# Summing the modulation over partitions as two rows on the two column halves of TensorE, spread by DMA over a scratch in DRAM

## Chip, core and metric

The kernel runs on one core of a Trainium2 chip. The metric is the device time of one execution in microseconds (us). A core has TensorE (PE, matrix products), VectorE (DVE), ScalarE (ACT), GpSimd (POOL) and SyncE (SP); SP, ACT and POOL issue DMAs, which all run on the core's 16 DMA engines.

## The reference, cut to what matters

The program is three transformer layers on 256 tokens of width 1024. The first layer has two feed-forward networks (FFN 0 and 1); the second and the third have one each (FFN 2 and 3) and are modulated by a condition vector `c`:

```
cond = jax.nn.silu(c)
for i in range(DEPTH_2):
    mod = (cond @ ada_w[i] + ada_b[i])[:, None, :]
    sh1, sc1, g1, sh2, sc2, g2 = jnp.split(mod, 6, axis=-1)
    h = rmsnorm_2(x, norm1_g[i]) * (1.0 + sc1) + sh1
    ...
    x = x + g1 * y
    h = rmsnorm_2(x, norm2_g[i]) * (1.0 + sc2) + sh2
    x = x + g2 * swiglu_2(h, w_gate[i], w_up[i], w_down[i])
```

`mod` is 12 parts of 1024 numbers (two layers of six). Eight of them (shifts and scales) are used per channel and four (gates) multiply rows of tokens.

## The kernel before

**Weights.** All layers' weights stream in 190 units of 128x2048 numbers (1 MB). For each unit SP issues the load, ACT rounds it to fp32r (`hi`, L465), DVE computes the rest (`lo`, L1094), and PE multiplies with both: `hi*x_hi + hi*x_lo + lo*x_hi` (L1878 to L1887). ACT and DVE work four units (`AHEAD`) ahead of PE.

**Pairs.** An FFN has 11 pairs `p` of three units. In a pair PE does the gate and up products for both token tiles (`gate_up`, 48 matmuls of 512 columns), turns the hidden values of the pair before (`turn_hid`, L2010), multiplies them into the output (`down_all`, 24 matmuls), and then does `mod_job(p)` if there is one. `down_all` waits for `hid_lo` (L1254) of DVE, which waits for `hid_hi` (L542) of ACT.  The next pair's first matmul waits for `hid_done` of this pair.

**Modulation.** POOL loads `ada_w` in 96 slices of 128x1024. DVE's `ada(n)` (L1105, L1109) multiplies slice `n` by its column of `cond` and adds it to `ada_acc[:, q % 2, :]`; after eight slices each partition holds a partial sum of part `q`, and what is left is the sum over the 128 partitions. This is done in PSUM bank 3 at the pairs that `MOD_JOBS` names, half a part (512 columns) at a time, so there are 24 jobs in pairs 4 to 9 of FFN 0 and at like places in FFN 1 to 3 (the fourth part of each group falls in pairs 2 and 3 of the next FFN):

- a shift or a scale: four PE transposes of 128x128 (L2045), after which DVE sums along the row (L1124), so that the numbers come out one per partition, and adds the bias (L1128);
- a gate: ACT rounds the whole `ada_acc` part to fp32r (L555), DVE computes the rest (L1274), PE multiplies both with a matrix of ones (L2040, L2041), so that all 128 partitions hold the sum, and DVE adds it to `gate` (L1120).

**Order.** Every engine's order is written out by hand, and engines meet at semaphores. `mod_ps` counts PE's jobs, `mod_read` DVE's reading of bank 3. A block's sum in front of a norm or a gated add is waited for by `modg_done` or `mod_read`, many pairs later.

Of the kernel before, what the change touches and what calls it, by code (L numbers as in the profile page):

```python
# [13 lines left out]
P = 128  # L14
T = 256
# [91 lines left out]
ADA_FROM, ADA_PAIRS = 2, 8  # L107
GATES = [q for q in range(ADA_PARTS) if q % 6 in GATE]
MOD_JOBS = {}
for _q in range(ADA_PARTS):  # L110
    _f, _i = _q // 4, _q % 4
    for _half in range(2):
        MOD_JOBS[(PAIRS * _f + 4 + 2 * _i if _i < 3 else PAIRS * (_f + 1) + 2) + _half] = (_q, _half)

# [74 lines left out]
def program(nc, inp, out):  # L189
    with ExitStack() as ctx:  # L190
# [28 lines left out]
        stat = sb("stat", [P, 3, 16])  # L219
        ones_r = sb("ones_r", [P, P], F32R)  # L220
        both = stat[:, 0, 12:16]
# [25 lines left out]
        xn = overlay("xn", 56 * T, [P, 2, D])  # L247
        acc_hi = overlay("acc_hi", 50 * T, [P, D], F32R)
        acc_lo = overlay("acc_lo", 56 * T, [P, D], F32R)
        y_tok = overlay("y_tok", 0, [P, 2, 16, HD])  # L250
# [45 lines left out]
        hi_ready, lo_ready, unit_done = sem("hi_ready"), sem("lo_ready"), sem("unit_done")  # L296
        ada_used, acc_hi_done, acc_lo_done, ones_set = sem("ada_used"), sem("acc_hi_done"), sem("acc_lo_done"), sem("ones_set")
        ident_in, const_in, dist_in, mask2_in = sem("ident_in"), sem("const_in"), sem("dist_in"), sem("mask2_in")
# [11 lines left out]
        proj_out, low_out = sem("proj_out"), sem("low_out")  # L310
        mod_ps, mod_read, mod_bias, modg_done = sem("mod_ps"), sem("mod_read"), sem("mod_bias"), sem("modg_done")
        up_done, value_done = sem("up_done"), sem("value_done")
# [56 lines left out]
        def ada_of_pair(g):  # L369
# [5 lines left out]
            return range(first, first + ADA_PER)  # L375

        def gate_of_pair(g):


            q, h = MOD_JOBS.get(g, (0, 1))  # L380
            return q if h == 0 and q % 6 in GATE else None

# [60 lines left out]
        def _(act):  # L443
# [5 lines left out]
            def late_inputs():  # L449
                act.activation(ones_r[:, :], ones, ACT.Copy).then_inc(ones_set, 1)  # L450
                act.dma_start(const[:, C_DIST:], inp["const"][:, C_DIST:]).then_inc(dist_in, 16)
                act.dma_start(sinks[:, :], inp["sinks"].partition_broadcast(P)).then_inc(sinks_in, 16)
                act.dma_start(pos_i[:, :], inp["positions"]).then_inc(pos_in, 16)
                for i, name in enumerate(("q_gain", "k_gain")):
                    act.dma_start(qk_gain[:, i, :], inp[name].partition_broadcast(P)).then_inc(sinks_in, 16)
                for i, q in enumerate(GATE):
                    act.dma_start(gate[:, i, :], inp["ada_b"][0][q * D:(q + 1) * D].partition_broadcast(P)) \
                        .then_inc(gate_in[i], 16)
# [65 lines left out]
            def ffn(f, n, then):  # L524
# [15 lines left out]
                def hid_hi_of(p, cols, count):  # L540
                    act.wait_ge(hidT_done, count)
                    act.activation(hid_hi[:, p % 2, cols], ps[:, 2, cols], ACT.Copy).then_inc(hidhi_done, 1)  # L542

                def pair(p):
                    ug, ud = ffn_gate(f, p), ffn_down(f, p - 1)
                    if p > 0:
                        hid_hi_of(p - 1, slice(0, 2 * T), hidT_count(f, p - 1) + 1)
                    hi(ug + AHEAD)
                    silu(p, 0)
                    silu(p, 1)  # L550
                    hi(ug + 1 + AHEAD)
                    q = gate_of_pair(f * PAIRS + p)
                    if q is not None:
                        act.wait_ge(ada_used, C * (q + 1))
                        act.activation(acc_hi[:, :], ada_acc[:, q % 2, :], ACT.Copy).then_inc(acc_hi_done, 1)  # L555
                    if p > 0:
                        hi(ud + AHEAD)

                u0 = BASE[f"ffn{f}"]
# [527 lines left out]
        def _(dve):  # L1087
# [9 lines left out]
            def ada(n):  # L1097

                q, k = n // C, n % C
                dve.wait_ge(ada_loaded[n % ADA_SLOTS], 16 * (n // ADA_SLOTS + 1))  # L1100
                acc = ada_acc[:, q % 2, :]
                if k == 0:
                    if q >= 2:
                        dve.wait_ge(mod_ps, 2 * (q - 1))
                    V.tensor_scalar(acc, ada_raw[:, n % ADA_SLOTS, :], cond[:, 0:1], None, ALU.mult) \  # L1105
                        .then_inc(ada_used, 1)
                else:
                    dve.wait_ge(ada_used, n)
                    V.scalar_tensor_tensor(acc, ada_raw[:, n % ADA_SLOTS, :], cond[:, k:k + 1], acc, ALU.mult,  # L1109
                                           ALU.add).then_inc(ada_used, 1)  # L1110

            def mod_job(q, h):

                layer, kind = q // 6, q % 6
                job = 2 * q + h
                dve.wait_ge(mod_ps, job + 1)
                if kind in GATE:
                    i = GATE.index(kind)
                    dve.wait_ge(gate_in[i], 16 * (layer + 1))
                    V.tensor_tensor(gate[:, i, half(h)], gate[:, i, half(h)], ps[:, 3, :], ALU.add) \  # L1120
                        .then_inc(mod_read, 1)
                    return
                part = slice(8 * kind + 4 * h, 8 * kind + 4 * h + 4)
                V.tensor_reduce(mod[:, layer, part], ps[:, 3, :].rearrange("p (t n) -> p t n", t=4), AX.X, ALU.add) \  # L1124
                    .then_inc(mod_read, 1)
                dve.wait_ge(mod_read, job + 1)
                bias = ada_bT[:, 48 * layer + part.start:48 * layer + part.stop]
                V.tensor_tensor(mod[:, layer, part], mod[:, layer, part], bias, ALU.add).then_inc(mod_bias, 1)  # L1128
                if kind in SCALE and h == 1:
                    which = SCALE.index(kind)  # L1130
                    dve.wait_ge(mod_bias, 8 * layer + 4 * which + 4)
                    V.scalar_tensor_tensor(mod_g[:, layer, which, :], mod[:, layer, 8 * kind:8 * kind + 8], 1.0,
                                           vec_t[:, 32 + 8 * layer + 16 * which:40 + 8 * layer + 16 * which], ALU.add,
# [99 lines left out]
            def ffn(f, n, then, factor=None, gated=None):  # L1233
# [23 lines left out]
                def modulation(p):  # L1257
                    if f * PAIRS + p in MOD_JOBS:
                        mod_job(*MOD_JOBS[f * PAIRS + p])

                def pair(p):
# [7 lines left out]
                    for k in units[0:1]:  # L1269
                        ada(k)  # L1270
                    q = gate_of_pair(f * PAIRS + p)
                    if q is not None:
                        dve.wait_ge(acc_hi_done, GATES.index(q) + 1)
                        V.tensor_tensor(acc_lo[:, :], ada_acc[:, q % 2, :], acc_hi[:, :].bitcast(F32), ALU.subtract) \  # L1274
                            .then_inc(acc_lo_done, 1)
                    for k in units[1:2]:
# [48 lines left out]
                if gated is not None:  # L1325
                    dve.wait_ge(mod_read, 2 * (6 * (f - 2) + GATE[1]) + 2)
                if then is not None and then not in UNSHIFTED:
# [42 lines left out]
            def rows_then(stage, n, gated=None):  # L1370
# [4 lines left out]
                if gated is not None:  # L1375
                    dve.wait_ge(mod_read, 2 * (6 + GATE[0]) + 2)
                    dve.wait_ge(modg_done, 4)
# [148 lines left out]
            def gqa():  # L1526
# [148 lines left out]
                lo(v0 + 4)  # L1675
                dve.wait_ge(mod_read, 2 * GATE[0] + 2)
                dve.wait_ge(modg_done, 2)
# [22 lines left out]
            def stick():  # L1700
# [80 lines left out]

                dve.wait_ge(mod_read, 2 * (6 + GATE[0]) + 2)
                dve.wait_ge(modg_done, 4)
# [88 lines left out]
        def _(pe):  # L1872
# [109 lines left out]
            def ffn(f, n, then):  # L1982
# [48 lines left out]
                def mod_job(p):  # L2031
                    if f * PAIRS + p not in MOD_JOBS:
                        return
                    q, h = MOD_JOBS[f * PAIRS + p]
                    pe.wait_ge(ada_used, C * (q + 1))
                    wait(pe, mod_read, 2 * q + h)
                    if q % 6 in GATE:
                        pe.wait_ge(ones_set, 1)
                        pe.wait_ge(acc_lo_done, GATES.index(q) + 1)
                        TE.matmul(ps[:, 3, :], ones_r[:, :], acc_hi[:, half(h)], start=True, stop=False)  # L2040
                        TE.matmul(ps[:, 3, :], ones_r[:, :], acc_lo[:, half(h)], start=False, stop=True) \  # L2041
                            .then_inc(mod_ps, 1)
                        return
                    for k in range(4):
                        m = TE.transpose(ps[:, 3, k * P:(k + 1) * P],  # L2045
                                         ada_acc[:, q % 2, h * HALF + k * P:h * HALF + (k + 1) * P], ident)
                    m.then_inc(mod_ps, 1)
# [586 lines left out]
```

## Time and profile before

| what | value |
|---|---|
| median of 3 runs (lowest to highest) | 1173.44 us (1173.38 to 1174.34) |
| the profiled execution's own time | 1174.04 us |
| its span, first to last instruction | 1172.2 us |
| PE busy | 1160.1 us, 99% |
| DVE busy | 820.6 us, 70% |
| ACT busy | 599.3 us, 51% |
| granted TensorE clock, mean | 0.999 of full |
| DMA moved | 253.66 MB, mean 216 GB/s |

The span runs from the first to the last instruction; the execution's own time has a little more around it. An engine that is busy for 99% of the span leaves no room for others to be the limit, except at the places where it waits. A PE matmul's duration in the rows holds its way through the array and overlaps the next one; what it costs is the distance from its start to the next one's start.

### The profile page before, as it was taken

To read this page: it belongs to the slowest core of one execution; us is meant where nothing else is said; L and a number is where in the kernel's file an instruction comes from. 1 tells how busy PE (TensorE), PEld (TensorE's weight loads), DVE (VectorE), ACT (ScalarE), POOL (GpSimd) and SP (SyncE) were. 2 spreads that over 40 slices of the span, in tenths; PEclk is the share of its full clock that TensorE was granted. 3 is DMA by queue.
4 is the path that set the end of the run, shared out by engine and by line. 5 is a ranking of instruction groups with operands and counts; after the bars stand their busy time and mean duration, and the time that the engine had idled before them with its cause. 6 is when DMAs were issued, how large, how long until landed. Compare 5 with 4: busy or idle time off the path is not lost. (4 is left out here: it accounts for less than half of the span.)

```text
span 1172.2 us, 15112 instructions
## 1 busy us (share of the span) xinstructions
PE 1160.1 (99%) x6140; PEld 978.5 (83%) x6140; DVE 820.6 (70%) x1051; ACT 599.3 (51%) x780; POOL 51.1 (4%) x101
## 2 busy tenths in 40 slices
PE   8999999999999999999999999999999999999998
PEld 6888888889989888888888888888888978888887
DVE  5777877456757657887898967788785658554544
ACT  7443356445566643353578544334565676433441
POOL 0011110000000001111000001111000000000000
PEclk9999999999999999999999999999999999999999
DMA  9888684554445578887624457887546405755530
GB/s 370 340 307 320 222 346 179 198 182 143 144 145 166 194 269 318 298 289 277 248 72 145 180 215 271 298 319 270 224 144 235 143 20 196 251 179 179 184 139 37
DMA packets 44421, 253.66 MB, mean 216 GB/s; under 512 B 5568, under 2 KB 5952, under 8 KB 20544
## 3 DMA queue, kind: packets, MB, share of 16 engines
q1 hardware_dynamic: 29088, 199.78, 46.9%
q0 software_dynamic: 13824, 50.34, 12.1%
q10 hardware_dynamic: 1440, 2.58, 0.6%
q8 instruction: 49, 0.80, 0.3%
q14 instruction: 20, 0.16, 0.0%
HBM read 251.63 MB, written 1.05 MB: 216 GB/s over the span
## 5 line engine op out<-in xcount | busy, mean ns | idle before, releaser
L1094 DVE TENSOR_TENSOR w_lo<-raw,w_hi 128x2048 fp32r<-128x2048 f32 x145 | 330.8, 2288 | 101.0 <-ACT w_hi L465 100.9
L465 ACT ACTIVATE w_hi<-raw 128x2048 fp32r<-128x2048 f32 x145 | 275.3, 1911 | 32.8 <-DMA raw<-in_w 32.6
L1885 PE MATMUL ps<-w_hi,h_parts 128*128 128x512 f32 (+1 forms) x720 | 284.2, 395 | 1.0 <-DVE h_parts L1218 0.5
L1887 PE MATMUL ps<-w_lo,h_parts 128*128 128x512 f32 (+1 forms) x720 | 277.8, 386 | 0.0
L1886 PE MATMUL ps<-w_hi,h_parts 128*128 128x512 f32 (+1 forms) x720 | 277.3, 385 | 0.0
L542 ACT ACTIVATE hid_hi<-ps 128x512 fp32r<-128x512 f32 (+1 forms) x48 | 27.0, 562 | 260.3 <-PE ps L2010 260.3
L1885 PEld LDWEIGHTS ps<-w_hi,h_parts 128*128 128x128 f32 x720 | 135.5, 188 | 27.7 <-DVE h_parts L1229 0.9
L1887 PEld LDWEIGHTS ps<-w_lo,h_parts 128*128 128x128 f32 x720 | 135.3, 188 | 27.9
L1886 PEld LDWEIGHTS ps<-w_hi,h_parts 128*128 128x128 f32 x720 | 135.8, 189 | 25.0
L1109 DVE SCALAR_TENSOR_TENSOR ada_acc<-ada_raw,cond,ada_acc 128x1024 f32<-128x1024 f32 x84 | 107.5, 1280 | 3.4 <-DMA ada_raw<-in_ada_w 1.2
L1094 DVE TENSOR_TENSOR lo_extra<-raw_extra,hi_extra 128x2048 fp32r<-128x2048 f32 x40 | 91.5, 2287 | 13.6 <-ACT hi_extra L465 13.5
L1885 PE MATMUL ps<-w_hi,hid_hi 128*128 128x512 f32 x248 | 96.8, 390 | 0.0
L1887 PE MATMUL ps<-w_lo,hid_hi 128*128 128x512 f32 x248 | 96.6, 389 | 0.0
L1886 PE MATMUL ps<-w_hi,hid_lo 128*128 128x512 f32 x248 | 96.5, 389 | 0.0
L1254 DVE TENSOR_TENSOR hid_lo<-ps,hid_hi 128x512 fp32r<-128x512 f32 (+1 forms) x48 | 31.0, 645 | 90.0 <-ACT hid_hi L542 89.9
L438 POOL DMA_DIRECT2D ada_raw<-in_ada_w x96 | 50.8, 530 | 781.8 <-DVE ada_acc L1109 392.8
L1885 PE MATMUL ps<-hi_extra,h_parts 128*128 128x512 f32 x208 | 82.5, 397 | 0.0
L1887 PE MATMUL ps<-lo_extra,h_parts 128*128 128x512 f32 x208 | 81.2, 390 | 0.0
L1886 PE MATMUL ps<-hi_extra,h_parts 128*128 128x512 f32 x208 | 81.0, 390 | 0.0
L465 ACT ACTIVATE hi_extra<-raw_extra 128x2048 fp32r<-128x2048 f32 x40 | 76.2, 1912 | 6.7 <-DMA raw_extra<-in_w 6.7
L1878 PE MATMUL ps<-h_parts,w_hi 128*128 128x256 f32 x240 | 69.6, 290 | 0.0
L1879 PE MATMUL ps<-h_parts,w_hi 128*128 128x256 f32 x240 | 67.9, 283 | 0.0
(236 smaller groups left out, 1686.7 us busy)
## 6 DMA issues: line engine op xcount, KB each, us to landing
raw<-in_w SPq DMA_DIRECT2D x146, 1024.0 KB, 4.9
ada_raw<-in_ada_w POOLq DMA_DIRECT2D x96, 512.0 KB, 5.2
raw_extra<-in_w SPq DMA_DIRECT2D x40, 1024.0 KB, 5.1
raw<-in_w SPq DMA_DIRECT2D x4, 256.0 KB, 5.9
gate<-in_ada_b ACTq DMA_DIRECT2D x2, 512.0 KB, 12.3
gate<-in_ada_b SPq DMA_DIRECT2D x2, 512.0 KB, 5.9
out_x<-x SPq DMA_DIRECT2D x4, 256.0 KB, 2.0
const<-in_const ACTq DMA_DIRECT2D x1, 768.0 KB, 8.1
```

The lines of the kernel that those rows point to most:

```text
L438: pool.dma_start(ada_raw[:, n % ADA_SLOTS, :], w[:, k, (q % 6) * D:(q % 6 + 1) * D]) \
L465: act.activation(w_hi[SLOT[u]], raw[SLOT[u]], ACT.Copy).then_inc(hi_ready, 1)
L542: act.activation(hid_hi[:, p % 2, cols], ps[:, 2, cols], ACT.Copy).then_inc(hidhi_done, 1)
L1094: V.tensor_tensor(w_lo[SLOT[u]], raw[SLOT[u]], w_hi[SLOT[u]].bitcast(F32), ALU.subtract) \
L1109: V.scalar_tensor_tensor(acc, ada_raw[:, n % ADA_SLOTS, :], cond[:, k:k + 1], acc, ALU.mult, ALU.add).then_inc(ada_used, 1)
L1254: V.tensor_tensor(hid_lo[:, p % 2, cols], ps[:, 2, cols], hid_hi[:, p % 2, cols].bitcast(F32), ALU.subtract).then_inc(hidlo_done, 1)
L1878: TE.matmul(dst, wh, x_hi, start=start, stop=False, skip_group_check=True)
L1879: TE.matmul(dst, wh, x_lo, start=False, stop=False, skip_group_check=True)
L1885: TE.matmul(dst, x_hi, wh, start=start, stop=False, skip_group_check=True)
L1886: TE.matmul(dst, x_lo, wh, start=False, stop=False, skip_group_check=True)
L1887: return TE.matmul(dst, x_hi, wl, start=False, stop=last, skip_group_check=True)
```

## The change

The sum over partitions becomes one job per part, 12 in all, at the first of the two pairs where the part's halves were before. PE multiplies `ada_acc` (true fp32, both halves of the row) by a 128x64 block of ones: columns 0 to 511 on the left 64 columns of the array (PSUM partitions 0 to 63 of bank 3), columns 512 to 1023 on the right 64 (partitions 64 to 127). ACT copies the bank to `mod_row` and issues a DMA of partitions 0 and 64, that is the whole row of 1024, into a DRAM tensor `mod_rows`. In the next pair ACT issues the DMA that brings it back: for shifts and scales number `128*k + p` to partition `p`, column `k` (1024 pieces of 4 bytes), for gates the whole row to each of the 128 partitions (512 KB). At that pair's end DVE waits for it (`mod_in`) and adds the bias, or adds the row to `gate`. The fp32r rounding for gates, `ones_r`, the transposes and the sums along the row go.

```
-    for _half in range(2):
-        MOD_JOBS[(PAIRS * _f + 4 + 2 * _i if _i < 3 else PAIRS * (_f + 1) + 2) + _half] = (_q, _half)
+    MOD_JOBS[PAIRS * _f + 4 + 2 * _i if _i < 3 else PAIRS * (_f + 1) + 2] = _q
...
+        gate_rows = overlay("gate_rows", 50 * T, [P, D])
+        mod_row = overlay("mod_row", 54 * T, [P, HALF])
+        scratch = nc.dram_tensor("mod_rows", (ADA_PARTS, D), F32).ap()
...
             def late_inputs():
-                act.activation(ones_r[:, :], ones, ACT.Copy).then_inc(ones_set, 1)
...
+                def send_mod(q):
+                    act.wait_ge(mod_ps, q + 1)
+                    wait(act, mod_sent, 16 * q)
+                    act.activation(mod_row[:, :], ps[:, 3, :], ACT.Copy).then_inc(mod_copied, 1)
+                    act.wait_ge(mod_copied, q + 1)
+                    act.dma_start(scratch[q].rearrange("(s n) -> s n", s=2), mod_row[0:P:P // 2, :]).then_inc(mod_sent, 16)
+
+                def fetch_mod(q):
+                    act.wait_ge(mod_sent, 16 * (q + 1))
+                    layer, kind = q // 6, q % 6
+                    if kind in GATE:
+                        act.dma_start(gate_rows[:, :], scratch[q].partition_broadcast(P)).then_inc(mod_in, 16)
+                    else:
+                        act.dma_start(mod[:, layer, 8 * kind:8 * kind + 8], scratch[q].rearrange("(k p) -> p k", p=P),
+                                      allow_slow_non_contiguous=True).then_inc(mod_in, 16)
+
                 def pair(p):
...
                     hi(ug + AHEAD)
+                    if f * PAIRS + p - 1 in MOD_JOBS:
+                        fetch_mod(MOD_JOBS[f * PAIRS + p - 1])
                     silu(p, 0)
                     silu(p, 1)
                     hi(ug + 1 + AHEAD)
-                    q = gate_of_pair(f * PAIRS + p)
-                    if q is not None:
-                        act.wait_ge(ada_used, C * (q + 1))
-                        act.activation(acc_hi[:, :], ada_acc[:, q % 2, :], ACT.Copy).then_inc(acc_hi_done, 1)
                     if p > 0:
                         hi(ud + AHEAD)
+                    if f * PAIRS + p in MOD_JOBS:
+                        send_mod(MOD_JOBS[f * PAIRS + p])
...
-            def mod_job(q, h):
+            def mod_job(q):
...
-                dve.wait_ge(mod_ps, job + 1)
+                dve.wait_ge(mod_in, 16 * (q + 1))
                 if kind in GATE:
                     i = GATE.index(kind)
                     dve.wait_ge(gate_in[i], 16 * (layer + 1))
-                    V.tensor_tensor(gate[:, i, half(h)], gate[:, i, half(h)], ps[:, 3, :], ALU.add) \
-                        .then_inc(mod_read, 1)
+                    V.tensor_tensor(gate[:, i, :], gate[:, i, :], gate_rows[:, :], ALU.add).then_inc(mod_done, 1)
                     return
-                part = slice(8 * kind + 4 * h, 8 * kind + 4 * h + 4)
-                V.tensor_reduce(mod[:, layer, part], ps[:, 3, :].rearrange("p (t n) -> p t n", t=4), AX.X, ALU.add) \
-                    .then_inc(mod_read, 1)
...
+                part = slice(8 * kind, 8 * kind + 8)
...
                 def modulation(p):
-                    if f * PAIRS + p in MOD_JOBS:
-                        mod_job(*MOD_JOBS[f * PAIRS + p])
+                    if f * PAIRS + p - 1 in MOD_JOBS:
+                        mod_job(MOD_JOBS[f * PAIRS + p - 1])
...
-                    q = gate_of_pair(f * PAIRS + p)
-                    if q is not None:
-                        dve.wait_ge(acc_hi_done, GATES.index(q) + 1)
-                        V.tensor_tensor(acc_lo[:, :], ada_acc[:, q % 2, :], acc_hi[:, :].bitcast(F32), ALU.subtract) \
-                            .then_inc(acc_lo_done, 1)
...
-                    q, h = MOD_JOBS[f * PAIRS + p]
+                    q = MOD_JOBS[f * PAIRS + p]
                     pe.wait_ge(ada_used, C * (q + 1))
-                    wait(pe, mod_read, 2 * q + h)
-                    if q % 6 in GATE:
-                        pe.wait_ge(ones_set, 1)
-                        pe.wait_ge(acc_lo_done, GATES.index(q) + 1)
-                        TE.matmul(ps[:, 3, :], ones_r[:, :], acc_hi[:, half(h)], start=True, stop=False)
-                        TE.matmul(ps[:, 3, :], ones_r[:, :], acc_lo[:, half(h)], start=False, stop=True) \
-                            .then_inc(mod_ps, 1)
-                        return
-                    for k in range(4):
-                        m = TE.transpose(ps[:, 3, k * P:(k + 1) * P],
-                                         ada_acc[:, q % 2, h * HALF + k * P:h * HALF + (k + 1) * P], ident)
+                    pe.wait_ge(const_in, 16)
+                    wait(pe, mod_copied, q)
+                    for h in range(2):
+                        m = TE.matmul(ps[h * HD:(h + 1) * HD, 3, :], ones[:, 0:HD], ada_acc[:, q % 2, half(h)],
+                                      start=True, stop=True, skip_group_check=True)
                     m.then_inc(mod_ps, 1)
```

The later waits on `mod_read` become waits on `mod_done`, which counts the 12 parts.

PE's row at the end of pair 4 of FFN 0, where part 0 has its first job, reads so before (the last matmuls of `down_all`, the job, the first of the next pair):

```order
L1885 MATMUL ps<-hi_extra_70,hid_hi 128x512
L1886 MATMUL ps<-hi_extra_70,hid_lo 128x512
L1887 MATMUL ps<-lo_extra_68,hid_hi 128x512
L2045 MATMUL ps<-const,ada_acc 128x128 [waits ada_used]
L2045 MATMUL ps<-const,ada_acc 128x128 x3
L1885 MATMUL ps<-w_hi,h_parts 128x512 [waits hid_done,lo_ready]
```

The same place in the changed kernel, where line numbers above the job are two higher (L1885 is L1887):

```order
L1887 MATMUL ps<-hi_extra_70,hid_hi 128x512
L1888 MATMUL ps<-hi_extra_70,hid_lo 128x512
L1889 MATMUL ps<-lo_extra_68,hid_hi 128x512
L2041 MATMUL ps<-ada_acc,const 64x512 [waits const_in,ada_used]
L2041 MATMUL ps<-ada_acc,const 64x512
L1887 MATMUL ps<-w_hi,h_parts 128x512 [waits hid_done,lo_ready]
```

Four transposes here and four in pair 5 have become the two matmuls here; pair 5 has none.

ACT's row around the boundary of pairs 4 and 5, before (the two last `hi` of pair 4, then pair 5):

```order
L465 ACTIVATE w_hi<-raw 128x2048 [waits w_loaded2]
L465 ACTIVATE w_hi<-raw 128x2048 [waits w_loaded3]
L542 ACTIVATE hid_hi<-ps 128x512 [waits hidT_done]
L465 ACTIVATE w_hi<-raw 128x2048 [waits w_loaded4]
L537 ACTIVATE silu_g<-ps,rstd 128x256 [waits hid_done,gu0_done]
```

The same place in the changed kernel (lines are eight lower here):

```order
L457 ACTIVATE w_hi<-raw 128x2048 [waits w_loaded2]
L457 ACTIVATE w_hi<-raw 128x2048 [waits w_loaded3]
L541 ACTIVATE mod_row<-ps 128x512 [waits mod_ps]
L543 DMA mod_rows<-mod_row 2x512 [waits mod_copied]
L534 ACTIVATE hid_hi<-ps 128x512 [waits hidT_done]
L457 ACTIVATE w_hi<-raw 128x2048 [waits w_loaded4]
L553 DMA mod<-mod_rows 128x8x1 [waits mod_sent]
L529 ACTIVATE silu_g<-ps,rstd 128x256 [waits hid_done,gu0_done]
```

The copy and the send stand ahead of `hid_hi`, the fetch ahead of the first `silu`.

## Rows read from the trace of the kernel before

**Rows 1.** The page: span, and PE's busy time, share and instructions.

```profile
span 1172.2 us, 15112 instructions
...
PE 1160.1 (99%) x6140; PEld 978.5 (83%) x6140; DVE 820.6 (70%) x1051; ACT 599.3 (51%) x780; POOL 51.1 (4%) x101
```

**Rows 2.** Waits: PE's longest; us in total, times, longest.

```profile
PE ps L1936 <- DMA x<-in_x: 5.1, 1, 5.1
```

**Rows 3.** Groups of PE by form: count, busy us, mean ns, idle before.

```profile
L2045 PE MATMUL ps<-const,ada_acc 128*128 128x128 f32 x64 | 9.6, 271 | 0.0
...
L2040 PE MATMUL ps<-acc_hi,ones_r 128*128 128x512 f32 x8 | 3.3, 407 | 0.0
```

**Rows 4.** Timeline of PE, a transposing job: start us, duration us, line.

```profile
89.48 0.39 PE L1887 MATMUL ps<-lo_extra,hid_hi 128*128 128x512 f32 x1
89.71 0.60 PE L2045 MATMUL ps<-const,ada_acc 128*128 128x128 f32 x4
...
90.38 0.40 PE L1886 MATMUL ps<-w_hi,h_parts 128*128 128x512 f32 x1
```

**Rows 5.** Timeline of PE around the first and the second gate job.

```profile
158.63 0.39 PE L1887 MATMUL ps<-w_lo,hid_hi 128*128 128x512 f32 x1
...
159.57 0.40 PE L1885 MATMUL ps<-w_hi,h_parts 128*128 128x512 f32 x1
...
176.17 0.39 PE L1887 MATMUL ps<-w_lo,hid_hi 128*128 128x512 f32 x1
...
176.86 0.39 PE L1885 MATMUL ps<-w_hi,h_parts 128*128 128x512 f32 x1
```

**Rows 6.** Timeline of PE, a visit to two column halves in fp32 (128*64).

```profile
930.08 0.28 PE L1879 MATMUL ps<-h_parts,w_hi 128*128 128x256 f32 x1
930.20 0.28 PE L1880 MATMUL ps<-h_parts,w_lo 128*128 128x256 f32 x1
930.41 0.65 PE L2413 MATMUL ps<-z_buf,qkv 128*64 128x256 f32 x4
930.90 0.39 PE L2417 MATMUL ps<-z_buf,qkv 128*64 128x128 f32 x4
931.21 0.39 PE L1878 MATMUL ps<-h_parts,w_hi 128*128 128x256 f32 x1
931.44 0.28 PE L1879 MATMUL ps<-h_parts,w_hi 128*128 128x256 f32 x1
```

**Rows 7.** Timeline of PE, both halves apart (probT one, soft the other).

```profile
318.48 0.38 PE L2187 MATMUL ps<-probT,qkv 128*64 128x256 f32 x1
318.48 0.38 PE L2187 MATMUL ps<-soft,qkv 128*64 128x256 f32 x1
...
318.91 0.27 PE L2191 MATMUL ps<-probT,qkv 128*64 128x128 f32 x1
```

**Rows 8.** Timeline of ACT, start of pair 5 of FFN 0.

```profile
96.28 0.60 ACT L542 ACTIVATE hid_hi<-ps 128x512 fp32r<-128x512 f32 x1 [7.72 <-PE ps L2010]
```

**Rows 9.** Timeline of DVE, end of pair 5 and start of pair 6.

```profile
112.10 0.68 DVE L1124 TENSOR_REDUCE mod<-ps 128x4 f32<-128x512 f32 x1
...
114.19 0.69 DVE L1254 TENSOR_TENSOR hid_lo<-ps,hid_hi 128x512 fp32r<-128x512 f32 x1 [1.22 <-ACT hid_hi L542]
```

**Rows 10.** Timeline of PE, the first matmul of `down_all` in pair 6.

```profile
118.84 0.39 PE L1885 MATMUL ps<-hi_extra,hid_hi 128*128 128x512 f32 x1
```

**Rows 11.** Timeline of ACT's queue: start and duration of two DMA issues.

```profile
35.16 0.55 ACTq L453 DMA_DIRECT2D pos_i<-in_positions  x1
...
36.71 0.33 ACTq L455 DMA_DIRECT2D qk_gain<-in_k_gain  x1
```

**Rows 12.** DMA issues: count, KB each, median us to landing.

```profile
gate<-in_ada_b ACTq DMA_DIRECT2D x2, 512.0 KB, 12.3
...
qk_gain<-in_k_gain ACTq DMA_DIRECT2D x1, 32.0 KB, 8.6
...
pos_i<-in_positions ACTq DMA_DIRECT2D x1, 1.0 KB, 7.8
```

More of the change, by code:

```diff
@@ L107 @@
 ADA_FROM, ADA_PAIRS = 2, 8
-GATES = [q for q in range(ADA_PARTS) if q % 6 in GATE]
 MOD_JOBS = {}
@@ L219, in program @@
         stat = sb("stat", [P, 3, 16])
-        ones_r = sb("ones_r", [P, P], F32R)
         both = stat[:, 0, 12:16]
@@ L247, in program @@
         xn = overlay("xn", 56 * T, [P, 2, D])
-        acc_hi = overlay("acc_hi", 50 * T, [P, D], F32R)
-        acc_lo = overlay("acc_lo", 56 * T, [P, D], F32R)
+        gate_rows = overlay("gate_rows", 50 * T, [P, D])
+        mod_row = overlay("mod_row", 54 * T, [P, HALF])
+        scratch = nc.dram_tensor("mod_rows", (ADA_PARTS, D), F32).ap()
         y_tok = overlay("y_tok", 0, [P, 2, 16, HD])
@@ L296, in program @@
         hi_ready, lo_ready, unit_done = sem("hi_ready"), sem("lo_ready"), sem("unit_done")
-        ada_used, acc_hi_done, acc_lo_done, ones_set = sem("ada_used"), sem("acc_hi_done"), sem("acc_lo_done"), sem("ones_set")
+        ada_used = sem("ada_used")
         ident_in, const_in, dist_in, mask2_in = sem("ident_in"), sem("const_in"), sem("dist_in"), sem("mask2_in")
@@ L310, in program @@
         proj_out, low_out = sem("proj_out"), sem("low_out")
-        mod_ps, mod_read, mod_bias, modg_done = sem("mod_ps"), sem("mod_read"), sem("mod_bias"), sem("modg_done")
+        mod_ps, mod_copied, mod_sent, mod_in = sem("mod_ps"), sem("mod_copied"), sem("mod_sent"), sem("mod_in")
+        mod_done, modg_done = sem("mod_done"), sem("modg_done")
         up_done, value_done = sem("up_done"), sem("value_done")
@@ L375, in ada_of_pair @@
             return range(first, first + ADA_PER)
-        def gate_of_pair(g):
-            q, h = MOD_JOBS.get(g, (0, 1))
-            return q if h == 0 and q % 6 in GATE else None
         @block.sync
@@ L1103, in ada @@
                     if q >= 2:
-                        dve.wait_ge(mod_ps, 2 * (q - 1))
+                        dve.wait_ge(mod_ps, q - 1)
                     V.tensor_scalar(acc, ada_raw[:, n % ADA_SLOTS, :], cond[:, 0:1], None, ALU.mult) \
@@ L1110, in ada @@
                                            ALU.add).then_inc(ada_used, 1)
-            def mod_job(q, h):
+            def mod_job(q):
                 layer, kind = q // 6, q % 6
-                job = 2 * q + h
-                dve.wait_ge(mod_ps, job + 1)
+                dve.wait_ge(mod_in, 16 * (q + 1))
                 if kind in GATE:
@@ L1119, in mod_job @@
                     dve.wait_ge(gate_in[i], 16 * (layer + 1))
-                    V.tensor_tensor(gate[:, i, half(h)], gate[:, i, half(h)], ps[:, 3, :], ALU.add) \
-                        .then_inc(mod_read, 1)
+                    V.tensor_tensor(gate[:, i, :], gate[:, i, :], gate_rows[:, :], ALU.add).then_inc(mod_done, 1)
                     return
-                part = slice(8 * kind + 4 * h, 8 * kind + 4 * h + 4)
-                V.tensor_reduce(mod[:, layer, part], ps[:, 3, :].rearrange("p (t n) -> p t n", t=4), AX.X, ALU.add) \
-                    .then_inc(mod_read, 1)
-                dve.wait_ge(mod_read, job + 1)
+                part = slice(8 * kind, 8 * kind + 8)
                 bias = ada_bT[:, 48 * layer + part.start:48 * layer + part.stop]
-                V.tensor_tensor(mod[:, layer, part], mod[:, layer, part], bias, ALU.add).then_inc(mod_bias, 1)
-                if kind in SCALE and h == 1:
+                V.tensor_tensor(mod[:, layer, part], mod[:, layer, part], bias, ALU.add).then_inc(mod_done, 1)
+                if kind in SCALE:
                     which = SCALE.index(kind)
-                    dve.wait_ge(mod_bias, 8 * layer + 4 * which + 4)
-                    V.scalar_tensor_tensor(mod_g[:, layer, which, :], mod[:, layer, 8 * kind:8 * kind + 8], 1.0,
+                    dve.wait_ge(mod_done, q + 1)
+                    V.scalar_tensor_tensor(mod_g[:, layer, which, :], mod[:, layer, part], 1.0,
                                            vec_t[:, 32 + 8 * layer + 16 * which:40 + 8 * layer + 16 * which], ALU.add,
@@ L1325, in ffn @@
                 if gated is not None:
-                    dve.wait_ge(mod_read, 2 * (6 * (f - 2) + GATE[1]) + 2)
+                    dve.wait_ge(mod_done, 6 * (f - 2) + GATE[1] + 1)
                 if then is not None and then not in UNSHIFTED:
@@ L1375, in rows_then @@
                 if gated is not None:
-                    dve.wait_ge(mod_read, 2 * (6 + GATE[0]) + 2)
+                    dve.wait_ge(mod_done, 6 + GATE[0] + 1)
                     dve.wait_ge(modg_done, 4)
@@ L1675, in gqa @@
                 lo(v0 + 4)
-                dve.wait_ge(mod_read, 2 * GATE[0] + 2)
+                dve.wait_ge(mod_done, GATE[0] + 1)
                 dve.wait_ge(modg_done, 2)
@@ L1780, in stick @@
                 y_lo(7)
-                dve.wait_ge(mod_read, 2 * (6 + GATE[0]) + 2)
+                dve.wait_ge(mod_done, 6 + GATE[0] + 1)
                 dve.wait_ge(modg_done, 4)
```

## The prediction

> **What bounds the kernel now.** I read the page first: PE is busy for 1160.1 of the 1172.2 us of the span [rows 1]. The reader is to see that about 12 us are all that PE could ever stop waiting for. The list of waits is next: PE's longest is 5.1 us for the first input, at the very start [rows 2]; nothing in the middle is of that size. So the time is PE's row of work, placed end to end, and the change is worth what it does to the length of that row, plus any wait that it newly gives to PE. DVE (70% busy) and ACT (51%) [rows 1] stand in the shadow of PE, and work taken from them is worth nothing.
>
> **What the removed PE work cost.** A job cannot be priced by its busy time, since matmuls overlap; I take distances between starts. Two fp32r matmuls of 512 columns and one more before them take 0.69 us from 176.17 to 176.86 [rows 5], so one is 0.23. A transposing job: from 89.48 to 90.38 are 0.90 us [rows 4], in which lie two ordinary matmuls (L1887 before, L1885 behind) of 0.23 each; the four transposes with what they do to their neighbours cost 0.44. There are 64 transposes [rows 3], that is 16 jobs: 7.0 us. A gate job: 8 of them [rows 3], seven at 0.46 and the first, where PE waited a little for the fp32r parts of `ada_acc`, at 0.94 less 0.23, or 0.71 [rows 5]: 3.9 us. Removed in all: **11.0 us**.
>
> **What the added PE work costs.** 12 jobs of two true-fp32 matmuls, 64 columns wide, 512 columns long, on the two halves. No such job with 512 columns is in the trace, but the form with 256 and 128 is, in both attention stages. First, how fast they stream: with both halves at work, two records of 256 columns on each half take 0.43 us, from 318.48 to 318.91 [rows 7]; that is four passes over 256 columns, and the two halves start at the same 318.48, so they run side by side and the second is free. 512 columns are twice that: 0.86 us a job. Second, what a visit to the halves costs beside streaming: from 930.20 to 931.44 are 1.24 us [rows 6]. In it lie two ordinary matmuls of 256 columns at 0.12 (930.08 to 930.20), streams of 256 columns (0.43) and of 128 (half of it, 0.215). 1.24 - 0.24 - 0.43 - 0.215 leaves 0.355 us: the array is let run empty on the way in and on the way out, and the weights of the first matmul on each side are not loaded under the one before. A job is 0.86 + 0.355 = 1.215 us, and 12 of them **14.6 us**.
>
> The Trainium skill, TensorEngine Tiling (Array Packing), section Key Properties, says that "Mode switching requires drain". The trace agrees with it by the 0.355 us of [rows 6]; the page gives no time for it. By the page's rule on concurrency alone, without the drain, the job would be 0.86 and the change a gain of 0.7 us; the trace has a price for the drain, and I use it.
>
> Bounds of a job: 0.86 us if the switches cost nothing here, which [rows 6] speaks against; 1.72 + 0.355 = 2.075 us if the halves take turns, which [rows 7] speaks against. The switching part itself may differ by the neighbours, which here are 512 columns long and not 256: after the transposes, L1885 also starts its follower late, within the 0.44 above, so a known part of such a loss is around 0.1. I let the job range from 1.12 to 1.31.
>
> **Sum.** 14.6 - 11.0 = +3.6 us on PE's row. The profiled execution took 1174.04 us with its span of 1172.2; it would take 1177.6. It lies 0.6 above the median of the runs, 1173.44, which is the spread between runs, so the median goes to **1177.0**.
>
> **What lies beside PE and is costed at nothing.** Twelve copies of 128x512 from PSUM on ACT, each like `hid_hi` at 0.60 us, and the issue of the send. They stand in front of `hid_hi` of the next pair. ACT had been idle for 7.72 us there, waiting for PE's turn of the hidden values [rows 8]. PE's job ends about when the 90.38 of [rows 4] stands, so copy and send are over by about 92.5, and behind them only `hid_hi` waits, due at 96.28. If that cover were gone, ACT would still have silu, `hi` and the 5 us of `down_all` between itself and PE. The fetch is issued behind `hi`; a DMA issue took ACT's queue 0.33 and 0.55 us [rows 11] and runs while ACT's `hi` is at work. Before, ACT and DVE also made the fp32r parts of gates, and DVE the sums of 0.68 us [rows 9]; their going frees DVE and moves nothing. SP's and POOL's queues are passed by no instruction; POOL's next slices are released by the same `ada` work as before.
>
> **The new wait on DVE.** At the end of the pair after the job DVE waits for the fetched row. What queues behind it: `hid_lo` of the next pair, and for that PE's `down_all`. For part 0 the fetch goes out just behind 96.28, say at 97.0 [rows 8]; DVE comes to its wait at 112.10 and next has work at 114.19 [rows 9]; PE needs `hid_lo`, 0.69 us long, at 118.84 [rows 10]. So a landing within 15 us costs nothing at all, and one within 21 us (118.1) nothing on PE. How long it takes: no transfer of 1024 pieces of 4 bytes is in the trace. From below it is a small transfer's time; the one of positions, 128 pieces, landed after 7.8 us, and the last gain, 128 pieces, after 8.6 [rows 12], both behind larger ones on the same queue. From above: positions landed at 35.16 + 7.8 = 42.96, the last gain at 36.71 + 8.6 = 45.3 [rows 11, 12], and between them 256 pieces, so at most 2.35 us / 256 = 9.2 ns each. 1024 pieces are 9.4 us, and 8.6 + 9.4 = 18.0 us if the queues are as full as there. That is under 21. I take no cost on PE. For the four gates the 512 KB broadcast has its like, 12.3 us to landing [rows 12], within 15 too.
>
> **Rivals.**
> - *The halves take turns.* 12 x 2.075 = 24.9 us, +13.9: 1187.3. Against it stands [rows 7]. For it only that 512 columns with one common operand were never seen. Chance 0.05.
> - *The fetch comes late.* The trace never showed pieces of 4 bytes in such number among weight loads. It decides from 21 us after the issue on; at 25 us PE would stand still for 4 us at each of the 8 shifts and scales, +32 and with the PE part about 1209; at 22 us it would be +8 and 1185. The page DMA: Bandwidth & Descriptors of the Trainium skill, section Rules for kernel authors, says that a non-contiguous last dim "Lowers to one descriptor per element", and its section Queues, rings and completion order that an engine changes between queues packet by packet. By that each small piece could stand behind a large one of the weights, which is this rival; [rows 12] shows small ones not that slow, though with fewer pieces. Chance 0.10.
> - *Not slower: the switches are hidden.* If weights were preloaded and the array not emptied between these neighbours, a job is 0.86 us, 12 are 10.3, and the change is -0.7: 1172.8, no change that could be told. It decides where the switching falls below about 0.25 us a job (then the change is under +2.35). [rows 6] is a visit with waits on both sides, so some of its 0.355 could belong to these. Chance 0.14.
> - *Faster by more than 0.2%* needs under 0.72 us a job, less than streaming alone. Or PE's remaining waits would have to go with DVE's relief, and there are hardly any [rows 2]. Chance 0.03.
> - The forecast as told: 0.68, with its own range from 1175.8 to 1178.4.
>
> **How the numbers follow.** A difference of 0.2% (2.35 us) is about what a measurement can tell from none. Slower: the forecast's 0.68, less 0.03 for its lower edge, with 0.05 and 0.10 of the two slow rivals: 0.80. Within: 0.14 + 0.03: 0.17. Faster: 0.03. The range leaves out the rival of turns (0.05), the half of the late fetch that costs more than 4 us (0.05), and most of the hidden switches with the faster end (0.10): 1174.3 to 1181.0.
>
> **What the changed profile would show.** The new matmul group has 48 records, in fours that start in twos, and from the last ordinary matmul of `down_all` to the second one behind the job some 1.7 us (1.215 and two of 0.23) where a transposing job had 0.90. Pairs 5, 7, 9 have no job. PE waits for nothing new; DVE's wait for the fetch is short or absent; the transfer's landing is under 15 us. The prediction is wrong if the records of the two halves lie behind each other, if the distance is nearer 1.3, or if `down_all` starts late in pairs 6, 8 and 10 with DVE's modulation named ahead of it.

## The result and the profile after

| what | before | after |
|---|---|---|
| median (lowest to highest), 8 runs each | 1173.53 us (1173.27 to 1174.34) | 1177.46 us (1176.39 to 1181.57) |
| ratio, 95% interval | | 1.0036 (1.0024 to 1.0048) |
| profiled execution, its span | 1174.04 us, 1172.2 us | 1177.57 us, 1175.5 us |

The changed kernel is slower by 3.9 us of the medians; 1177.46 was measured where 1177.0 was forecast. Its times spread wider: two of the eight are 1179.48 and 1181.57, the other six, its main group, lie from 1176.39 to 1177.98 with a median of 1177.09, which is 3.6 us above the kernel before.

The page of the changed kernel, which answers to [rows 1]: span, busy time with share and instructions, and the DMA share of the span in tenths.

```profile
span 1175.5 us, 15035 instructions
PE 1163.4 (99%) x6108; PEld 971.3 (83%) x6108; DVE 804.8 (68%) x1019; ACT 602.3 (51%) x787; POOL 51.1 (4%) x101
...
DMA  9888694554444578887624457887636405755540
```

PE's busy time grew by 3.3 us (1160.1 to 1163.4) and the span by 3.3. DVE has 16 us less to do, and the span did not get shorter by it. PE is still the whole length of the span, so the place to look is its own row.

The timeline of PE of the changed kernel at the end of pair 4 (start, duration, line), which answers to [rows 4]. L1889 is the last matmul of `down_all`, L2041 the job with two records for each of its two matmuls.

```profile
89.73 0.39 PE L1889 MATMUL ps<-lo_extra,hid_hi 128*128 128x512 f32 x1
90.05 1.08 PE L2041 MATMUL ps<-ada_acc,const 128*64 128x512 f32 x4
91.06 0.50 PE L1887 MATMUL ps<-w_hi,h_parts 128*128 128x512 f32 x1
91.39 0.39 PE L1888 MATMUL ps<-w_hi,h_parts 128*128 128x512 f32 x1
```

From 89.73 to 91.39 are 1.66 us; less two ordinary matmuls of 0.23 that is 1.20 us for the job. The forecast had 1.215. All twelve jobs read the same, 1.66 or 1.67 us. The three parts of the loss can be read here too: L2041 starts 0.32 behind L1889 and not 0.23; L1887 starts 1.01 behind it and not 0.86; L1888 starts 0.33 behind L1887 and not 0.23. That is 0.09 + 0.15 + 0.10 = 0.34 us.

The transfers, in the list of DMA issues of the changed kernel (count, KB each, median us to landing), answer to [rows 12]. The new wait of DVE does not appear in its list of waits. The small pieces can be counted in the page: packets under 512 B went from 5568 to 13976, and 8192 of these 8408 are eight fetches of 1024.

```profile
gate_rows<-mod_rows ACTq DMA_DIRECT2D x4, 512.0 KB, 8.3
...
mod_rows<-mod_row ACTq DMA_DIRECT2D x12, 4.0 KB
...
mod<-mod_rows ACTq DMA_DIRECT2D x8, 4.0 KB, 6.7
```

The view of the instructions that write `mod` gives the shortest, median and longest landing of the eight fetches of 4-byte pieces:

```profile
DMA to landing us min/median/max: 2.3/6.7/12.3
```

The longest, 12.3 us, is the fetch of part 6, issued at 554.37 in pair 9 of FFN 1. The other seven took 2.3 to 7.1 us. The experiments come back to the fetch of 12.3 us.

### The profile page after: what moved, and what is told of

Its sections match the earlier page's. It is cut to its first block and busy times, and to the rows that moved or that the text cites. A ratio compares the mean times of both kernels' runs of the same rounds, so it can differ in the third digit from the quotient of the medians.

```text
span 1175.5 us, 15035 instructions
## 1 busy us (share of the span) xinstructions
PE 1163.4 (99%) x6108; PEld 971.3 (83%) x6108; DVE 804.8 (68%) x1019; ACT 602.3 (51%) x787; POOL 51.1 (4%) x101
## 2 busy tenths in 40 slices
DMA packets 53365, 255.84 MB, mean 218 GB/s; under 512 B 13976, under 2 KB 14360, under 8 KB 29488
## 3 DMA queue, kind: packets, MB, share of 16 engines
q0 software_dynamic: 13824, 50.34, 12.3%
## 5 line engine op out<-in xcount | busy, mean ns | idle before, releaser
L1887 PE MATMUL ps<-w_hi,h_parts 128*128 128x512 f32 (+1 forms) x720 | 284.3, 395 | 1.0 <-DVE h_parts L1236 0.5
L1889 PE MATMUL ps<-w_lo,h_parts 128*128 128x512 f32 (+1 forms) x720 | 278.1, 386 | 0.0
L1888 PE MATMUL ps<-w_hi,h_parts 128*128 128x512 f32 (+1 forms) x720 | 277.6, 386 | 0.0
L1887 PEld LDWEIGHTS ps<-w_hi,h_parts 128*128 128x128 f32 x720 | 135.7, 189 | 34.1 <-issue 7.3
L1889 PEld LDWEIGHTS ps<-w_lo,h_parts 128*128 128x128 f32 x720 | 135.4, 188 | 27.8
L1888 PEld LDWEIGHTS ps<-w_hi,h_parts 128*128 128x128 f32 x720 | 135.8, 189 | 24.9
L1887 PE MATMUL ps<-w_hi,hid_hi 128*128 128x512 f32 x248 | 96.9, 391 | 0.0
L1888 PE MATMUL ps<-w_hi,hid_lo 128*128 128x512 f32 x248 | 96.6, 390 | 0.0
L1889 PE MATMUL ps<-w_lo,hid_hi 128*128 128x512 f32 x248 | 96.6, 389 | 0.0
L1887 PE MATMUL ps<-hi_extra,h_parts 128*128 128x512 f32 x208 | 82.6, 397 | 0.0
L1889 PE MATMUL ps<-lo_extra,h_parts 128*128 128x512 f32 x208 | 81.2, 391 | 0.0
L1888 PE MATMUL ps<-hi_extra,h_parts 128*128 128x512 f32 x208 | 81.1, 390 | 0.0
```

The costliest lines, as they stand in the source:

```text
L1887: TE.matmul(dst, x_hi, wh, start=start, stop=False, skip_group_check=True)
L1888: TE.matmul(dst, x_lo, wh, start=False, stop=False, skip_group_check=True)
L1889: return TE.matmul(dst, x_hi, wl, start=False, stop=last, skip_group_check=True)
```

## Experiments

Theory: the whole cost is PE's twelve visits to the column halves, 1.20 us each against 11.0 us removed. Rival: part of the cost, or of the spread, is in the transfers and the wait for them. A difference between two experiments is taken between their medians on the same chip, unless said otherwise.

### Transfers out

The edit is cut to what matters here. DVE's adds stay and take what is in place, `gate` to itself and the bias to itself.

```
-                    act.wait_ge(mod_copied, q + 1)
-                    act.dma_start(scratch[q]...mod_row[0:P:P // 2, :]).then_inc(mod_sent, 16)
...                  (fetch_mod is empty)
-                dve.wait_ge(mod_in, 16 * (q + 1))
+                dve.wait_ge(mod_copied, q + 1)
```

> Left out: the send to DRAM and the fetch back; the modulation then consists of biases alone, and ACT's copy out of PSUM stays. Theory (all of the change's cost is PE's twelve visits to the column halves): the transfers were in the shadow of PE, so this takes the time of the changed kernel, 1177.0 to 1177.6, and its span is within 0.5 us of 1175.5. Rival (part of the cost is the transfers or what waits for them): it takes less, 1174 to 1176, and the spread of its runs is as small as that of the kernel before.

Measured: 1176.93 us (1176.66 to 1177.90, seven runs), ratio to before 1.0029 (1.0019 to 1.0040), span 1174.9. So in an ordinary execution the transfers cost about nothing: 1176.9 lies inside the changed kernel's main group of 1176.4 to 1178.0. The median lies 0.1 under the expected 1177.0 to 1177.6 and the span 0.6 from 1175.5, where 0.5 was allowed, so the expectation was just missed; the 1174 to 1176 of the rival were not reached either. But the rival had one thing right: without transfers the times near 1180 are gone. Seven runs against two high ones in eight did not settle that by themselves.

### No job on PE

`mod_job` of PE returns at once; ACT's and DVE's waits for `mod_ps` go too.

> Left out: PE's matmuls of the twelve jobs and the waits for them; ACT copies and sends whatever stands in the bank, and DVE fetches it, so all transfers stay. Theory: the time falls from the changed kernel's by 12 x 1.20 = 14.4 us, to about 1163.0. Rival (waits for transfers cost part): it falls by 12 to 13 us only from the same start if they still cost, to above 1164.5; or PE's visits cost more around them than the 1.20 us between neighbours, and it falls below 1162.

Measured: 1167.97 us (1167.05 to 1169.63, five runs). The 1163.0 of the theory was missed by 5 us. The rival's mark, above 1164.5, was passed, though not by its account: the time fell by 9.5 us from the changed kernel's median and not by 12 to 13. The time that is missing had to be a new wait of PE. The list of waits of this kernel (who waited for whom: us, times, longest) has it, beside PE's start and behind a wait of DVE:

```profile
DVE mod L1132 <- DMA mod<-mod_rows: 5.0, 1, 5.0
...
PE ps L1884 <- DVE hid_lo L1258: 3.7, 1, 3.7
```

That is 3.7 of the 5 us; where the rest went is read below, in the whole-array kernel.

### Both matmuls on the same half

```
-                        m = TE.matmul(ps[h * HD:(h + 1) * HD, 3, :], ones[:, 0:HD], ...
+                        m = TE.matmul(ps[0:HD, 3, :], ones[:, 0:HD], ...
```

> Changed: both matmuls of a job write the left half of the array, so the second one replaces the first one's result and the row of 1024 is not whole. Theory (the two halves stream side by side, and the second matmul was free): they now take turns, and each job costs 0.86 us more, 12 x 0.86 = +10.3 us, to about 1187.5, with eight starts one behind the other. Rival (the halves already took turns in part): it costs 5 us or less more.

Measured: 1187.15 us (1186.65 to 1187.43, four runs), ratio 1.0114 (1.0101 to 1.0127). The timeline of PE at the same job:

```profile
89.28 0.39 PE L1889 MATMUL ps<-lo_extra,hid_hi 128*128 128x512 f32 x1
89.59 1.93 PE L2041 MATMUL ps<-ada_acc,const 128*64 128x512 f32 x4
91.45 0.50 PE L1887 MATMUL ps<-w_hi,h_parts 128*128 128x512 f32 x1
91.80 0.40 PE L1888 MATMUL ps<-w_hi,h_parts 128*128 128x512 f32 x1
```

2.52 us less 0.46 is 2.06 a job, 0.86 more than on two halves. The second half was free in the change, as [rows 7] had it; and 1187.15 is what the rival "the halves take turns" was priced at (1187.3).

### The whole array, one matmul

```
-                    for h in range(2):
-                        m = TE.matmul(ps[h * HD:(h + 1) * HD, 3, :], ones[:, 0:HD], ada_acc[:, q % 2, half(h)],
+                    m = TE.matmul(ps[:, 3, :], ones, ada_acc[:, q % 2, half(0)],
```

> Changed: one true-fp32 matmul of 512 columns on the whole array in place of the two on halves, so columns 512 to 1023 of each part are left out. It streams as long as the pair did, but never changes the array's shape. Theory (about 0.25 us or more of a job is the change of shape): a job costs 0.86 to 0.95 us, and the time is 12 x 0.25 to 0.34 = 3.0 to 4.1 us under the changed kernel, 1173.4 to 1174.5. Rival (the loss at the borders belongs to true fp32 beside fp32r, not to the halves): a job costs 1.15 to 1.20 us and the time stays at 1176.8 to 1177.5.

Measured: twelve runs in two groups, seven from 1172.26 to 1173.24 and five from 1176.48 to 1178.45, with nothing between. The profiled execution (span 1176.1) is of the upper one. Its timeline of PE has the job:

```profile
89.24 0.39 PE L1889 MATMUL ps<-lo_extra,hid_hi 128*128 128x512 f32 x1
89.47 1.02 PE L2040 MATMUL ps<-ada_acc,const 128*128 128x512 f32 x2
89.92 0.80 PE L1887 MATMUL ps<-w_hi,h_parts 128*128 128x512 f32 x1
90.56 0.40 PE L1888 MATMUL ps<-w_hi,h_parts 128*128 128x512 f32 x1
```

1.32 less 0.46 is 0.86 us: the streaming alone, on fp32 between fp32r matmuls, with no loss. So the 0.34 us belongs to the change of the array's shape and not to the change of data type. 12 x 0.34 is 4.1 us. The median of the lower group, 1172.71, lies 4.4 under that of the changed kernel's main group (1177.09) and 4.2 under the kernel without transfers. It is 0.7 below the expected 1173.4 to 1174.5, which had been counted from 1177.46 with its two high runs.

The upper group shows the other cost. Here are three views of this execution, of ACT's queue, DVE and PE in pairs 9 and 10 of FFN 1 (in brackets: idle before it, and for what):

```profile
551.53 0.36 ACTq L553 DMA_DIRECT2D mod<-mod_rows  x1
```

```profile
570.89 0.17 DVE L1135 TENSOR_TENSOR mod<-mod,vecs 128x8 f32<-128x8 f32 x1 [4.67 <-DMA mod<-mod_rows]
570.98 0.68 DVE L1261 TENSOR_TENSOR hid_lo<-ps,hid_hi 128x512 fp32r<-128x512 f32 x1
```

```profile
567.95 0.39 PE L1889 MATMUL ps<-w_lo,h_parts 128*128 128x512 f32 x1
571.71 0.50 PE L1887 MATMUL ps<-hi_extra,hid_hi 128*128 128x512 f32 x1 [3.38 <-DVE hid_lo L1261]
...
574.65 0.63 PE L1889 MATMUL ps<-lo_extra,hid_hi 128*128 128x512 f32 x1
575.08 0.63 PE L1887 MATMUL ps<-hi_extra,hid_hi 128*128 128x512 f32 x1
...
579.14 0.39 PE L1887 MATMUL ps<-w_hi,h_parts 128*128 128x512 f32 x1
```

The fetch lands after 19.3 us, DVE stands still for 4.67 with `hid_lo` behind it, and PE goes on at 571.71. It would have gone on at 568.18 (567.95 + 0.23), so the wait itself costs 3.5 us. With 0.69 for `hid_lo`, the landing had to be there by about 567.5, 16 us after the issue.

The wait costs more than itself. From 571.71 to the first matmul of the next weights at 579.14 are 7.43 us; in the whole-array kernel without the wait, two experiments further on, the same work takes 5.76. The windows view (busy us of each engine, granted clock, DMA share, GB/s) has the reason for the other 1.7 us:

```profile
571.70:573.00 1.30, 1.29 (x6) 1.07 (x7) 0.35 (x1) 0.00 (x0) 0.00 (x0) 1.00 0.00 0
573.00:576.40 3.40, 3.40 (x11) 2.62 (x10) 1.95 (x2) 2.37 (x3) 0.00 (x0) 0.50 0.00 0
```

PE stood idle, ran for 1.3 us at the full granted clock, and then had half of it, 1.2 and not 2.4 GHz, for 3.4 us, in which matmuls start 0.43 apart and not 0.23. Together the late fetch costs 5.2 us, and the medians of the two groups (1172.71 and 1177.99) lie 5.3 apart. The kernel without a PE job shows the same: 3.8 us until PE goes on at 565.83, then 7.42 where 5.76 are usual, 5.5 us in all.

In the stretch from 552 to 562 the DMA engines are full; the same view shows a share of 1.03 there, against 0.82 in the stretch of the first fetch:

```profile
97.00:107.00 10.00, 10.00 (x46) 8.28 (x45) 7.78 (x7) 6.41 (x6) 1.05 (x2) 1.00 0.82 271
...
552.00:562.00 10.00, 10.00 (x45) 8.26 (x44) 7.71 (x7) 6.49 (x6) 1.05 (x2) 1.00 1.03 385
```

The changed kernel's own traced execution has the same 1.03 in this stretch and the landing at 12.3 us, so a full stretch goes with a late landing but does not decide between 12 and 19.

### The adds of pair 9 later

```
                 def modulation(p):
+                    if later and p == 9:
+                        return
...
+                if later:
+                    mod_job(MOD_JOBS[f * PAIRS + 8])
```

`later` holds in FFN 1 and 2; the second piece stands at the FFN's very end.

> Changed: for the parts fetched in pair 9 of FFN 1 and of FFN 2, DVE's wait and bias add move behind the FFN's last pair; PE's jobs, sends and fetches stay. Theory (the high ones among the changed kernel's times, 1179.5 and 1181.6, come from the one fetch of FFN 1 pair 9, which took 12.3 to 19.3 us to land against 2.3 to 9 for the others, in front of DVE's hid_lo): those times go, all runs lie within 1176.3 to 1178.0 and the median is 1176.8. Rival (the spread is from weight loads or elsewhere): runs above 1178.5 stay.

Measured: 1176.67 us (1176.48 to 1177.44, nine runs), ratio 1.0024 (1.0014 to 1.0033). The runs near 1180 are gone. Nine runs against two high ones in eight make that likely to be the edit's work, and do not prove it.

The same edit on the whole-array kernel, which had shown the two groups far more often:

> Changed: the full-width kernel (columns 512 to 1023 of each part left out) with the same adds moved behind the last pair. The full-width kernel had 5 of 12 runs at 1176.5 to 1178.5 and 7 at 1172.3 to 1173.2, and a profiled one in which PE waited 3.4 us for hid_lo behind that fetch. Theory: all runs are at 1172.2 to 1173.3, and PE waits for no hid_lo beyond 0.3 us. Rival: the upper group stays.

Measured: 1172.88 us, all eleven runs from 1172.44 to 1173.30. The upper group is gone, though the fetch is as late as before. Here are the landing line of `mod` in this kernel, the only wait for `hid_lo` that is left on PE's side (one weight load's), and PE's row at the place of the wait:

```profile
DMA to landing us min/median/max: 2.7/7.1/19.0
```

```profile
PEld ps L1893 <- DVE hid_lo L1261: 0.3, 1, 0.3
```

```profile
568.39 0.39 PE L1893 MATMUL ps<-hi_extra,hid_hi 128*128 128x512 f32 x1
...
574.15 0.39 PE L1893 MATMUL ps<-w_hi,h_parts 128*128 128x512 f32 x1
```

So the upper group is the wait, with what the clock does behind it, and not the transfer.

### Back to no job on PE

> Left out: PE's matmuls of the twelve jobs and the waits for them, as in the kernel without a PE job, and now the adds of the parts fetched in pair 9 stand behind the FFN's last pair. Theory (the kernel without a PE job missed its 1163.0 by 5 us because PE waited 3.7 us behind the late fetch in every run): it now takes 12 x 1.20 = 14.4 us less than the add-later kernel's 1176.7, 1162.3 to 1162.9. Rival (a job costs PE less than the distances between its neighbours say): it stays above 1164.

Measured: 1162.38 us (1162.09 to 1162.70). From the add-later kernel that is 14.3 us for twelve jobs (each against its own before, 1173.54 and 1173.74: 14.5), where the distances said 14.4. The earlier miss of 5 us was the late fetch: the wait and the slower clock behind it, 5.5 us by that kernel's rows. All five of its runs, from 1167.05 up, lie above the highest here, so it hit every one. In this kernel's trace the fetch landed after 19.7 us, and no engine waited for it. The kernel before stands 11.4 us above this one, where 11.0 was reckoned for its 24 jobs.

### Fewer, larger pieces

```
-                        act.dma_start(mod[...], scratch[q].rearrange("(k p) -> p k", p=P),
-                                      allow_slow_non_contiguous=True).then_inc(mod_in, 16)
+                        act.dma_start(mod[...], scratch[q].rearrange("(p k) -> p k", p=P)).then_inc(mod_in, 16)
```

> Changed: in the full-width kernel (columns 512 to 1023 of each part left out), whose DVE still waits in pair 9, the shifts and scales are fetched as 128 pieces of 32 bytes and not 1024 of 4, which puts them in another order (their channels are wrong). Theory A (the late fetch is late by the number of its pieces, each behind weights on the DMA engines): the fetch in FFN 1 pair 9 lands within 8 us, there are no runs near 1177 and the median is 1172.8. Theory B (any transfer on ACT's queue waits that long while the DMA engines are full): it still lands after 12 to 19 us, and about 5 of 12 runs are at 1176.5 to 1178.5.

Measured: 1172.64 us, all eleven runs from 1172.11 to 1173.19. The landing line of `mod`:

```profile
DMA to landing us min/median/max: 2.2/6.5/8.7
```

The one of pair 9 took the 8.7. Seven fetches took about as long as with 1024 pieces. The one of pair 9 had taken 9.4 to 19.7 us in the eight traces with pieces of 4 bytes, so 8.7 alone would say little; that none of eleven runs is in the upper group, where five of twelve were with 1024 pieces, says more. (They are from another chip than the twelve; on it the kernel without a PE job had its landing at 19.7.) So the count of pieces mattered where the DMA engines were full, and at none of the other seven places. This is theory A, except for its bound of 8 us.

### Quarters

```
+                    for h in range(4):
+                        m = TE.matmul(ps[h * 32:(h + 1) * 32, 3, 0:T], ones[:, 0:32],
+                                      ada_acc[:, q % 2, h * T:(h + 1) * T], start=True, stop=True,
+                                      skip_group_check=True)
...
+                    act.activation(mod_row[:, 0:T], ps[:, 3, 0:T], ACT.Copy).then_inc(mod_copied, 1)
...
+ ... scratch[q].rearrange("(s n) -> s n", s=4), mod_row[0:P:P // 4, 0:T]
```

> Changed: each job as four true-fp32 matmuls of 256 columns on four groups of 32 columns of the array, ACT copies 128x256, the send takes four partitions, and the adds are moved as in the add-later kernel. Nothing is left out. Theory (all groups stream side by side and a change of shape costs 0.34 us whatever the shape): a job costs 0.43 + 0.34 = 0.77 us, 12 of them 9.2 against 14.4, and the time is 5.2 us under the add-later kernel: 1171.6 to 1172.2, below the kernel before. Rival (four groups share something, as the operand's read, that two did not): they stream at half that rate, and it takes 1176.8 as the halves do.

Measured: 1171.21 us (1171.05 to 1172.03, eleven runs), ratio to before 0.9978 (0.9970 to 0.9987), which is 0.4 below the expected range. The timeline of PE at the job of pair 4:

```profile
88.89 0.39 PE L1895 MATMUL ps<-lo_extra,hid_hi 128*128 128x512 f32 x1
89.21 0.64 PE L2047 MATMUL ps<-ada_acc,const 128*32 128x256 f32 x8
89.78 0.50 PE L1893 MATMUL ps<-w_hi,h_parts 128*128 128x512 f32 x1
90.11 0.39 PE L1894 MATMUL ps<-w_hi,h_parts 128*128 128x512 f32 x1
```

1.22 less 0.46 is 0.76 us a job: half the streaming, 0.43, and the same 0.33 at the borders. Twelve are 9.1 us, 5.3 less than with halves; 5.5 were measured. It is the fastest complete kernel here, 2.3 us under the one before.

## Why the prediction was right, and where it was not

- **PE's row is the time.** Right. DVE's 16 us less of work gave nothing; what changed PE's row changed the time by the same amount (14.4 reckoned against 14.3 measured, 5.3 against 5.5, 10.3 against 10.5 from the add-later kernel).
- **Removed 11.0 us.** Right within 0.4: 11.1 by the distances at all 24 jobs before, 11.4 by the kernel without jobs.
- **Added 14.6 us: streaming 0.86 and 0.355 beside it.** Right: 0.86 and 0.34 by the timeline, and each half apart by an experiment of its own. The row of 256 columns held for 512, and the price of the visit taken from [rows 6] held between other neighbours. The rule of TensorEngine Tiling (Array Packing), Key Properties, in the Trainium skill, that a change of mode drains the array, agrees with the 0.34 us that only the kernels with another shape paid and the whole-array one did not.
- **The halves take turns (0.05).** Wrong, and its price right: 1187.15 when they are made to.
- **The switches are hidden (0.14).** Wrong: 0.34 each.
- **The new wait costs PE nothing.** Right for eleven of the twelve fetches, and not always for one. The step that failed is the bound "within 21 us": it was worked out at pair 6, where PE has 48 matmuls of `gate_up` ahead of `down_all`. In the last pair PE comes to `hid_lo` after half of them, and there the bound is about 16 us. The 18.0 us that the prediction allowed as the longest landing was over that, and was itself passed: 18.8, 19.3, 19.0 and 19.7 us in four traces. The rival "the fetch comes late" (0.10) therefore holds, at one place of eight.
- **What the wait costs when it comes.** The rival priced it as PE's standing still alone, 4 us at a landing of 25 us. The traced executions that had it lost 5.2 and 5.5 us at landings of 19.3 and 18.8: 3.5 and 3.8 of waiting, and 1.7 of half the granted clock behind it, a term that the prediction does not have.
- **The median escaped it, and that is luck.** It hit two of the changed kernel's eight runs, if their height is this wait. Had it hit most, as it did without the job, the median would have been about 1182 (1177.09 and 5.2, an estimate), beyond the 1181.0 of the range.

For the changed kernel no execution with the wait is in a trace: that its two high runs are this wait is inferred from their going away when the adds are moved. In the whole-array kernel and in the one without a PE job the wait was traced, and moving the adds took it and its cost away; there it is shown.

What stays open is why the landing of that fetch is at 9.4 to 12.3 us in some executions and at about 19 in others. The kernel that issues it first had it late in all five runs, the whole-array one in five of twelve, the changed kernel, which issues it last of the three, perhaps in two of eight. But the quarters kernel issues it at 550.57, before the whole-array one (551.53), and its traced landing is 11.4 us. So the time of the issue alone does not decide it, and how it falls among the weight loads was not separated by any run.

## What to carry to other kernels

Price a short matmul job by the distance between the starts of its neighbours, and split it into what streams and what the borders cost: here a change of the array's shape cost 0.34 us a visit however little was done in it, so the visit has to be rare or to save more than that. If the shape is changed at all, cut the job into more column groups, since two and four of them streamed side by side here. A wait that is harmless in the middle of a loop has to be checked again in the first and the last turn, where the engine behind it comes sooner. A wait of TensorE can cost more than its length: here 3.5 us of standing still brought 1.7 us more at half the clock. And one late transfer in one place shows first as a second group of run times.

## What was not expected of the hardware

- Four groups of 32 columns with four different operands stream at the full rate together: 256 columns in true fp32 on each take 0.43 us for all.
- True fp32 between fp32r matmuls of the same shape loses nothing: 0.86 us for 512 columns, four passes of 0.215.
- 4 KB in 1024 pieces landed as fast as in 128 pieces (6.7 and 6.5 us in the median) while the DMA engines had a little room, and at 12.3 to 19.3 against 8.7 us where their share was 1.03.
